# Attention and experts on one core: the head norms' inverse roots as a power on GpSimd, the copies of an even unit ahead of its exponentials, and two transpose groups an expert in place of four

## What is computed

```python
def hybrid_layer(x, ...):
    xn = rms_norm(x, norm1_w)
    hq, hf_f, hf_b, hi, hg, aq, ak, av = jnp.split(xn @ w_in, ...)
    o_hg = hgrn2_bidirectional(...)      # rms_norm(o_fwd + o_bwd, norm_w) * silu(hg), per head of 128
    o_da = diff_attention(...)           # softmax(s0) - lam * softmax(s1), @ v, rms_norm per head of 128
    h = x + jnp.concatenate([o_hg, o_da], -1) @ w_out
    return h + expert_choice_moe(rms_norm(h, norm2_w), router_w, w1, w3, w2)

def expert(w1e, w3e, w2e, ie, ge):       # 16 experts, 32 + 64 rows each, D_FF = 2816
    xe = jnp.take(xt, ie, axis=0)
    return (jax.nn.silu(xe @ w1e) * (xe @ w3e)) @ w2e * ge[:, None]
```

## Time and profile before

| | us |
|---|---|
| median of 3 runs | 2010.86 |
| lowest and highest | 2010.84, 2012.59 |
| the profiled execution: its own time | 2011.43 |
| the profiled execution: its span | 2009.6 |
| TensorE busy in the span | 1978.7 |
| VectorE busy | 1620.6 |
| ScalarE busy | 1302.5 |
| GpSimd busy | 81.0 |

### The profile page before, as it was taken

The page is one execution under the profiler, slowest core; times in us unless marked ns, Lnnn a source line. Parts: engine busy times, 40 slices in busy tenths (PEclk is TensorE's granted clock), DMA queues, the critical chain, the costliest instruction groups (busy, mean ns, idle before and its releaser), DMA issues.

```text
span 2009.6 us, 26132 instructions
## 1 busy us (share of the span) xinstructions
PE 1978.7 (98%) x9770; PEld 1656.9 (82%) x9770; DVE 1620.6 (81%) x1247; ACT 1302.5 (65%) x1000; POOL 81.0 (4%) x50
## 2 busy tenths in 40 slices
PE   9999999999899999999999999999999999999998
PEld 8888888878688888888888888888888888888886
DVE  5248877865888888888888888888888889888886
ACT  5234434743677777777777777777777777777774
POOL 0000000200000000000000000000000000000000
PEclk9999999999899999999999999999999999999999
DMA  5212314244799999999999999999999999999994
GB/s 163 64 53 84 111 68 147 85 148 178 290 391 365 401 365 391 375 385 388 374 393 374 402 359 405 362 390 378 383 388 380 390 371 399 360 405 364 392 380 159
DMA packets 217984, 615.98 MB, mean 307 GB/s; under 512 B 14833, under 2 KB 57073, under 8 KB 217938
## 3 DMA queue, kind: packets, MB, share of 16 engines
q1 hardware_dynamic: 214096, 602.70, 79.9%
q0 software_dynamic: 3696, 12.59, 2.7%
q10 hardware_dynamic: 146, 0.07, 0.0%
HBM read 595.66 MB, written 19.66 MB: 306 GB/s over the span
## 4 chain that ended last, share of the span: by engine, by line
PE 94%; DVE 3%; ACT 1%; DMA 1%; issue 1%; POOL 0%; ACTq 0%; POOLq 0%
PE pair L727 29%; PE pair L729 29%; PE pair L728 29%; PE pair L847 2%; PE pair L1207 1%; PE pair L917 1%; PE pair L1145 1%; PE pair L950 0%; PE pair L1039 0%; PE pair L897 0%; PE pair L937 0%; DMA raw_w<-w_in 0%; ACT probs L1379 0%; PE pair L879 0%; PE pair L980 0%
## 5 line engine op out<-in xcount | busy, mean ns | idle before, releaser
L2187 DVE TENSOR_TENSOR chunk_low<-ring,chunk_high 128x3072 fp32r<-128x3072 f32 (+1 forms) x384 | 1180.4, 3088 | 197.5 <-ACT chunk_high L1543 195.7
L1543 ACT ACTIVATE chunk_high<-ring 128x3072 fp32r<-128x3072 f32 (+1 forms) x384 | 983.3, 2569 | 329.6 <-PE pair L729 329.6
L727 PE MATMUL pair<-chunk_high,xe_high 128*128 128x512 f32 x1408 | 551.2, 391 | 1.0 <-DVE xe_low L2181 1.0
L729 PE MATMUL pair<-chunk_high,xe_low 128*128 128x512 f32 x1408 | 548.5, 390 | 0.0
L728 PE MATMUL pair<-chunk_low,xe_high 128*128 128x512 f32 x1408 | 547.7, 389 | 0.0
L729 PEld LDWEIGHTS pair<-chunk_high,xe_low 128*128 128x128 f32 x1408 | 264.3, 188 | 55.6
L727 PEld LDWEIGHTS pair<-chunk_high,xe_high 128*128 128x128 f32 x1408 | 264.4, 188 | 54.8 <-ACTq L1589 1.2
L728 PEld LDWEIGHTS pair<-chunk_low,xe_high 128*128 128x128 f32 x1408 | 264.5, 188 | 54.1
L727 PE MATMUL pair<-chunk_high,hid_high 128*128 128x512 f32 x704 | 276.9, 393 | 0.0
L729 PE MATMUL pair<-chunk_high,hid_low 128*128 128x512 f32 x704 | 274.5, 390 | 0.0
L728 PE MATMUL pair<-chunk_low,hid_high 128*128 128x512 f32 x704 | 274.0, 389 | 0.0
(11 more groups left out here) (265 smaller groups left out, 1776.7 us busy)
## 6 DMA issues: line engine op xcount, KB each, us to landing
ring<-w SPq DMA_DIRECT2D x240, 1536.0 KB, 8.9
ring<-w SPq DMA_DIRECT2D x128, 1024.0 KB, 8.7
ring<-w SPq DMA_DIRECT2D x32, 768.0 KB, 8.9
raw_w<-w_in SPq DMA_DIRECT2D x40, 256.0 KB, 2.9
ring<-w SPq DMA_DIRECT2D x32, 256.0 KB, 6.4
ring<-w SPq DMA_DIRECT2D x16, 512.0 KB, 10.0
raw_w<-w_in SPq DMA_DIRECT2D x6, 1024.0 KB, 5.4
wo_raw<-w_out SPq DMA_DIRECT2D x8, 512.0 KB, 3.6
```

Source lines behind the costliest of these rows:

```text
L727: pe.matmul(dst, a_high, b_high, start=first, stop=False)
L729: return pe.matmul(dst, a_low, b_high, start=False, stop=last)
L1543: act.activation(ch[c % SPLIT][:, 0:n], ring[c % RING][:, 0:n], ACT.Copy).then_inc(ch_done, 1)
L2187: dve.tensor_tensor(cl[c % SPLIT][:, 0:n], ring[c % RING][:, 0:n], ch[c % SPLIT][:, 0:n].bitcast(F32), ALU.subtract).then_inc(cl_done, 1)
```

## The change

First, `head_root` goes from ScalarE to GpSimd, which raises the mean to the power -0.5 with a tile of constants; the reciprocal on VectorE goes. Second, in the even steps ScalarE does the copy of unit a-2 ahead of the exponentials of unit a; in the odd steps the order stays. Third, the stops for transposes after chunks 7 and 13 become one after 13 (block 0's go to bank PD, block 1's to PC), and those after 17 and 20 become one after 17 (the next expert's rows go to bank PA). The splits of block 0 follow with chunk 14, of block 1 with chunk 15, of block 2 and of the rows with chunk 18. TensorE's waits move with them: chunk 0 now waits for both halves of `xe_low`, where chunk 1 waited for the second, and chunk 16 waits for block 0 and chunk 19 for block 1.

```diff
-HID_AT = {LAST[b, 1] + 2: b for b in range(NB)}
-XE_AT = len(UP) + 4
+HID_AT = {LAST[1, 1] + 2: (0, 1), LAST[2, 1] + 2: (2,)}
+HID_SPLIT_AT = {LAST[1, 1] + 3: 0, LAST[1, 1] + 4: 1, LAST[2, 1] + 3: 2}
+XE_AT = LAST[NB - 1, 1] + 2
...
+    minus_half = sb(perm, "minus_half", [P, TILES - 2, 8])
...
+        XB = (PA[:, 0:512], PA[:, 512:1024])
+        HB = (PD[:, 0:512], PD[:, 512:1024])
...
                     if c == 0:
                         pe.wait_ge(pads, 2)
-                        pe.wait_ge(tl_done, e * T_PER_EXPERT + 1)
-                    if c == 1:
                         pe.wait_ge(tl_done, e * T_PER_EXPERT + 2)
...
                     if j == 0:
                         pe.wait_ge(pads, 4)
-                        pe.wait_ge(y_ev, e + 1)
+                        pe.wait_ge(tl_done, e * T_PER_EXPERT + (2 + 2))
+                    if W2_AT[j] <= HALVES[1][0][0] < W2_AT[j] + W2_KT[j]:
                         pe.wait_ge(tl_done, e * T_PER_EXPERT + (2 + 4))
...
                 if c in HID_AT:
-                    b = HID_AT[c]
-                    pe.wait_ge(hid_done, e * NB + (b + 2))
-                    pe.wait_ge(tl_done, e * T_PER_EXPERT + (2 + 2 * b))
-                    for g, (k0, n) in enumerate(HALVES[b]):
-                        for i in range(n):
-                            mm = pe.transpose(TB[g][:, i * SLOTS:(i + 1) * SLOTS], hid[:, tile(k0 + i)],
-                                              ident[0:SLOTS, 0:SLOTS])
-                        mm.then_inc(t_mm, 1)
+                    for b in HID_AT[c]:
+                        pe.wait_ge(hid_done, e * NB + (b + 2))
+                        if b == 0:
+                            pe.wait_ge(y_ev, e + 1)
+                        if b == 2:
+                            pe.wait_ge(tl_done, e * T_PER_EXPERT + (2 + 4))
+                        for g, (k0, n) in enumerate(HALVES[b]):
+                            for i in range(n):
+                                mm = pe.transpose((HB if b == 0 else TB)[g][:, i * SLOTS:(i + 1) * SLOTS], hid[:, tile(k0 + i)],
+                                                  ident[0:SLOTS, 0:SLOTS])
+                            mm.then_inc(t_mm, 1)
                 if not last and c == XE_AT:
-                    pe.wait_ge(tl_done, e * T_PER_EXPERT + (2 + 2 * NB))
                     for j in range(2):
-                        transpose_rows(j, e * 16 + 32)
+                        transpose_rows(XB, j, e * 16 + 32)
...
         def head_root(group):
             own = NORM_TILES[group]
-            act.wait_ge(o_v, 2 * group + 1)
-            act.activation(head_rstd[:, own, :], head_ss[:, own, :], ACT.Sqrt).then_inc(o_std, 1)
...
+            if 2 <= a < ATT_UNITS + 2 and a % 2 == 0:
+                evac_probs(a - 2)
             if AHEAD <= a < ATT_UNITS:
                 exponentials(a)
-            if 2 <= a < ATT_UNITS + 2:
+            if 2 <= a < ATT_UNITS + 2 and a % 2 == 1:
                 evac_probs(a - 2)
-            if a == ROOT_AT:
-                head_root(0)
...
             dve.wait_ge(o_std, group + 1)
-            dve.reciprocal(head_rstd[:, tiles, :], head_rstd[:, tiles, :]).then_inc(o_v, 1)
-            dve.wait_ge(o_v, 2 * group + 2)
...
-                if c - 1 in HID_AT:
-                    b = HID_AT[c - 1]
+                if c in HID_SPLIT_AT:
+                    b = HID_SPLIT_AT[c]
...
+        def head_root(group):
+            own = NORM_TILES[group]
+            n = own.stop - own.start
+            pool.wait_ge(o_v, group + 1)
+            pool.tensor_tensor(head_rstd[:, own, :], head_ss[:, own, :], minus_half[:, 0:n, :], ALU.pow).then_inc(o_std, 1)
+
+        pool.memset(minus_half[:, :, :], -0.5)
         for a in range(ATT_UNITS + 4):
+            if a == ROOT_AT:
+                head_root(0)
...
+        head_root(1)
```

More of the change, by code:

```diff
@@ L1144, in transpose_rows @@
             for k in range(4):
-                mm = pe.transpose(TB[j][:, k * SLOTS:(k + 1) * SLOTS], xe[:, tile(4 * j + k)],
+                mm = pe.transpose(banks[j][:, k * SLOTS:(k + 1) * SLOTS], xe[:, tile(4 * j + k)],
                                   ident[0:SLOTS, 0:SLOTS])
@@ L1152, in _ @@
         for j in range(2):
-            transpose_rows(j, 16)
+            transpose_rows(TB, j, 16)
         def expert(e, last):
@@ L1531, in _, with rows_high @@
         TB = (PC[:, 0:512], PC[:, 512:1024])
-        def rows_high(j, value):
+        XB = (PA[:, 0:512], PA[:, 512:1024])
+        HB = (PD[:, 0:512], PD[:, 512:1024])
+        def rows_high(banks, j, value):
             act.wait_ge(t_mm, value)
-            act.activation(xeh[:, 4 * j:4 * j + 4, 0:SLOTS], TB[j][:, 0:4 * SLOTS].rearrange("p (k n) -> p k n", k=4),
+            act.activation(xeh[:, 4 * j:4 * j + 4, 0:SLOTS], banks[j][:, 0:4 * SLOTS].rearrange("p (k n) -> p k n", k=4),
                            ACT.Copy).then_inc(th_done, 1)
@@ L1559, in expert @@
                         act.activation(hid_h[:, k0:k0 + n, 0:SLOTS],
-                                       TB[g][:, 0:n * SLOTS].rearrange("p (k n) -> p k n", k=n),
+                                       (HB if b == 0 else TB)[g][:, 0:n * SLOTS].rearrange("p (k n) -> p k n", k=n),
                                        ACT.Copy).then_inc(th_done, 1)
@@ L1585, in _ @@
         act.wait_ge(route_done, 3)
-        rows_high(0, 1)
-        rows_high(1, 2)
+        rows_high(TB, 0, 1)
+        rows_high(TB, 1, 2)
         act.sem_inc(y_ev, 1)
@@ L2177, in _, with rows_low @@
         TB = (PC[:, 0:512], PC[:, 512:1024])
[L2179 removed]
+        XB = (PA[:, 0:512], PA[:, 512:1024])
+        HB = (PD[:, 0:512], PD[:, 512:1024])
+        def rows_low(banks, j, value):
             dve.wait_ge(th_done, value)
[L2181 removed]
+            dve.tensor_tensor(xel[:, 4 * j:4 * j + 4, 0:SLOTS], banks[j][:, 0:4 * SLOTS].rearrange("p (k n) -> p k n", k=4),
                               xeh[:, 4 * j:4 * j + 4, 0:SLOTS].bitcast(F32), ALU.subtract).then_inc(tl_done, 1)
@@ L2218, in _ @@
         dve.sem_inc(hid_done, 1)
-        rows_low(0, 1)
-        rows_low(1, 2)
+        rows_low(TB, 0, 1)
+        rows_low(TB, 1, 2)
         chunk_low(0, 1)
```

14 lines of the change are left out of this document (6 added, 8 removed).

## The result

The changed kernel takes 2016.44 us (median of 13 runs, 2015.14 to 2017.28), the kernel before on the same chip 2012.76 us (13 runs, 2010.76 to 2013.6). The ratio is 1.002, with a 95% interval from 1.0013 to 1.0028: slower by 0.2%, 3.7 us, where 5.8 us less had been forecast. One execution of those behind this document, the profiled one of experiment 1, took 4051.59 us, twice as long as any other; its trace isn't read.

A forecast was written before the change was run, and what follows sets the result against it. TensorE, busy 1978.7 of 2009.6 us, was taken as the bound. Attention 4.9, second root -0.5, transpose groups 1.9 and first expert's wait -0.5 sum to 5.8 us gained: median 2005.1 us, with 0.5 chance of 2003.0 to 2007.2.

The forecast's parts named there:

- the root on GpSimd: Head roots as GpSimd powers, 1.04 us each: first covered, second a 0.5 us loss (gain of 0.52 to loss of 1.4).
- a power much longer than 2 us: Sign in the profile after, at GpSimd's roots, that would show the forecast wrong.
- The copies before 365 us: Attention units: probability copy put ahead of a pair's exponentials removes two TensorE waits before 365 us, 1.2 us gained.
- No table load among the units: Attention units 14 to 16: two ScalarE table loads and the root leave the queue, 2.8 us gained (1.2 to 5.3).
- the wait for exponentials near 400 us: Sign that the forecast is right: TensorE waits 1 to 2 us for exponentials near 399 us.
- the 2.2 us on VectorE's path: Within the table-load term: earlier reduction, no reciprocal and a shorter 512-column product bring unit 16's maximum 2.2 us earlier.
- From unit 18 on: Attention pairs 18, 20 and 22: the copy leaves the chain, about 0.3 us each, 0.9 us gained (0 to 1.3).
- Two transpose groups: Expert loop: 32 transpose stops instead of 63 at 0.06 us each, 1.9 us gained (0 to 4.3).
- Rival 4: Expert loop: TensorE waits at chunk 18 in every expert, 11 us less 5.8 gained, 2016.5 us; chance 0.08.
- Rival 3: First power holds GpSimd some 6 us, so the reduction's 1.2 us are lost: 2006.3 us; chance 0.1.
- another drain of 1380 ns a load: Skill's rule for ScalarE table loads, 2.66 us a switch: another 2.8 us would leave ScalarE's queue; kept out of the sum.

The follow-up runs named there:

- experiment 1: Changed kernel with the second group's root back as ScalarE's Sqrt and VectorE's reciprocal, first power kept on GpSimd: 2009.01 us, ratio 0.9984 to the kernel before.
- experiment 6: Changed kernel with 24 filler products of 128 columns on TensorE ahead of the first logits: 2012.15 us, ratio 1.0002 to the kernel before.
- experiment 8: Changed kernel with the squares of the last gated tile and attention tile 2 on ScalarE, not GpSimd: 2014.77 us, ratio 1.0012 to the kernel before.
- Experiment 2: Kernel before with only both roots moved to GpSimd as powers: 2020.05 us, ratio 1.0038 to the kernel before.
- experiment 10: Changed kernel with the second root back on ScalarE and VectorE, chunk 0 waiting for the rows' first low half only, chunk 1 for the second: 2008.23 us, ratio 0.998.
- experiment 3: Kernel before with only the order of the copies in the even steps changed: 2011.11 us, ratio 0.999 to the kernel before.
- experiment 7: Changed kernel with the second power as four powers of 8 columns, each waited for by its own tile: 2011.11 us, ratio 0.9994 to the kernel before.
- experiment 4: Kernel before with only the two transpose groups an expert: 2011.41 us, ratio 0.9996 to the kernel before.
- experiment 9: Changed kernel with both roots back on ScalarE and VectorE, copies' order and transpose groups kept: 2010.33 us, ratio 0.9989 to the kernel before.
- experiment 11: Changed kernel with second root back, chunk 0's wait split, and squares of last gated tile and attention tile 2 on ScalarE: 2005.89 us, ratio 0.9969.

## Why the prediction was wrong

The step that failed is **the root on GpSimd**. It said that no row showed a power, took 1.04 us from the products of 512 columns, and set the upper end at 1.96 us, the longest of them. 5.43 us were measured. The bound was none: a product's cost for 512 columns says nothing of another function's cost for each column, and the text itself said "an unknown time per column". The prediction gave what would make it wrong, "a power much longer than 2 us", but its range had no term for it, and the one rival with a slow power put it at the first power, where it is covered, and not at the second, where nothing covers it. The term is 4.8 us where 0.5 was put.

**The clock behind that wait** was not in the sum at all. The prediction read it in the kernel before (2.42 us idle, then half speed), counted on winning it there, and didn't ask the same of the waits that the change makes longer. It cost 3.2 us behind the power (shown by experiment 6) and, in the traces, 1.6 us at the first expert. The wait there grew by 0.46 us (0.5 forecast), but its price was 2.1.

**The copies before 365 us:** 1.25 us for 1.2. Right.

**No table load among the units:** 0.63 us for 2.8, below the lower bound of 1.2. The mechanism was right (the loads are gone, the wait at L899 fell from 1.29 to 0.57, and the wait for exponentials near 400 us is 1.36, where 1 to 2 had been forecast). What failed is the 2.2 us on VectorE's path. Its maximum of unit 16 starts at 397.50, 0.99 us earlier than before, and 0.85 of these were had already ahead of this stretch: 0.14 us where 2.2 were booked. The sum let the product of 512 columns fall from 1.56 to 0.75 us "if GpSimd is not at work beside it", and it did (396.83, 0.75 us); but GpSimd's squares, which had stood beside that product, now stand beside VectorE's mix, and the mix became 1.6 us longer (experiment 8), for which the sum had no term. With the squares away, 0.63 + 1.6 = 2.2 us are won, by stretch I of experiment 8. Experiment 2 shows besides that without the copies ahead the loads' removal gains next to nothing (0.3 us).

**From unit 18 on:** 0.63 us for 0.9, within its bounds.

**Two transpose groups:** 2.8 us for 1.9, from 92.55 to 92.364 us an expert, where about 92.43 had been forecast. A stop that isn't made costs more than the 0.06 us taken, within the bounds.

**Rivals.** Rival 4's time, 2016.5 us, is the measured one by chance: its mechanism isn't there, it meant 5.6 us more than before where 3.7 were measured, and its own terms (11 us less 5.8) give 2016.1. No wait of TensorE stands in the loop after the first chunk, and chunk 18 was not late. Rival 3 had the power's slowness, about half as much as it supposed, at the place where it costs nothing. The Trainium skill's rule for it (GPSIMD Engine Reference, "Instruction dispatch", some 6 us for a first call of freshly loaded code) isn't borne out: the first power took 2.93 us and the second, with the code used already, 5.43, which goes by columns; nor had GpSimd stood idle ahead of the first (384.94, no idle time in its row). The Trainium skill's other rule that was weighed (ScalarE: Activation LUTs, "What ACT_TABLE_LOAD costs", another drain of 1380 ns a load) would have left more to win here than was forecast; less was won.

What stays open: why the clock falls behind the same waits in one execution and not in another. Two such places are the first expert (experiment 10) and the 0.78 us ahead of the first logits (experiment 3). Waits of some 0.6 and 1.9 us at 389 and 395 us stand in the changed kernel and in experiments 6, 7 and 10. From 390 to 400 us the clock was 1.00 in the changed kernel and in experiment 7, 0.83 in 6 and 10. That costs little where the next wait takes it up (0.4 us at L927 in experiment 10 instead of 1.36), but it makes single traces differ by a microsecond or two. That it is also what the medians' uncertainty of about 2 us comes from isn't shown. Open is also why GpSimd's squares slow VectorE's mix and its powers don't.

## What to carry to other kernels

When an operation moves to an engine where the trace has no instance of it, the row of another function is no bound, neither whole nor by the column: here a power costs 0.16 us a column and a product 0.002 (1.04 us for 512). Where the operation has no cover, measure it alone first, for it is the term that decides. Price a longer wait of TensorE twice, once as idle time and once as low clock behind it: here 4.8 us of wait cost another 3.2, and 0.5 us another 1.6 in five traces of seven. And when instructions move, look at what they come to stand beside: next to GpSimd's squares VectorE's mix took nearly twice its time.

## What the runs showed of the hardware

- A power of two tensors on GpSimd takes 1.66, 2.93 and 5.43 us for 8, 16 and 32 columns on 128 partitions: 0.16 us a column, against 1.04 us for a product of 512 columns.
- With GpSimd's squares beside them, VectorE's products of the mix took 1.91 and 1.52 us, without them 1.13 and 0.69, and beside GpSimd's powers 1.14 and 0.69 (experiment 7).
- A wait of 5.6 us was followed by 6.8 us of work at the lower clock in the changed kernel, 5.9 in experiment 8 and 8.8 in experiment 2; with TensorE kept at work through the same wait there were none. A wait of 0.78 us was followed by full clock in the kernel before and in experiments 4 and 9 to 11, and by a clock of 0.50 about 3 us later in experiment 3.
